# One of four weight sums moved from VectorE to GpSimd, and one product cut in two, in a decoder layer's MLP

## The reference

```python
u = rmsnorm(x, g_mlp[l]) @ w_up[l]
x = x + jnp.square(jax.nn.relu(u)) @ w_down[l]
return rmsnorm(x, g_final)
```

## Time and profile before

| | us |
|---|---|
| median of 3 runs | 415.57 (415.13 to 416.92) |
| the profiled execution, its own time | 416.76 |
| its span, first to last instruction | 415.0 |
| TensorE busy | 405.4 |
| VectorE busy | 333.9 |
| ScalarE busy | 250.4 |
| GpSimd busy | 27.0 |
| granted TensorE clock, mean share of full | 0.995 |

### The profile page before, as it was taken

How to read it: one execution, slowest core, us unless ns; L and a number is a source line. 1 busy time by engine, 2 the same in 40 slices (tenths; PEclk the granted TensorE clock), 3 DMA queues, 4 the chain that set the end, 5 groups by cost and what they waited for, 6 DMA issues and landing times.

```text
span 415.0 us, 7057 instructions
## 1 busy us (share of the span) xinstructions
PE 405.4 (98%) x2839; PEld 374.0 (90%) x2839; DVE 333.9 (80%) x441; ACT 250.4 (60%) x295; POOL 27.0 (6%) x40
## 2 busy tenths in 40 slices
PE   8999999999999999999999999999999999999993
PEld 7999988999999999889988899999999999999982
DVE  4788556977765737874858888999999999999976
ACT  5763337865665634551556648777777777777743
POOL 0079100000000000000200000000000000000003
PEclk9999999999999999999999999999999999999997
DMA  8999653534325255555453245555655555555002
GB/s 271 421 421 404 208 202 117 196 114 186 109 96 203 103 204 203 202 181 175 153 183 122 101 149 204 197 203 200 203 205 202 197 201 198 200 205 227 2 0 101
DMA packets 12107, 77.47 MB, mean 187 GB/s; under 512 B 1328, under 2 KB 1328, under 8 KB 3632
## 3 DMA queue, kind: packets, MB, share of 16 engines
q1 hardware_dynamic: 12080, 77.09, 51.7%
HBM read 76.04 MB, written 1.05 MB: 186 GB/s over the span
## 4 chain that ended last, share of the span: by engine, by line
PE 94%; DVE 2%; DMA 1%; ACT 1%; issue 0%; POOL 0%; SPq 0%; POOLq 0%; DVEq 0%; ACTq 0%
PE bank L1152 41%; PE bank L1447 16%; PE bank L1171 16%; PE bank L1288 11%; PE bank L1202 2%; PE bank L1300 1%; DVE res L1087 1%; DMA head_all<-in_pair_dram 1%; PE bank L1393 1%; PE bank L1413 1%; PE bank L1185 1%; PE bank L1341 1%; PE bank L1326 0%; PE bank L1406 0%; PE bank L1264 0%
## 5 line engine op out<-in xcount | busy, mean ns | idle before, releaser
L707 DVE TENSOR_TENSOR w_lo<-raw,w_hi 128x2048 fp32r<-128x2048 f32 (+2 forms) x83 | 145.0, 1753 | 26.5 <-ACT w_hi L455 25.2
L1152 PE MATMUL bank<-hT_hi,w_hi 128*128 128x256 f32 x384 | 108.2, 282 | 0.4 <-DVE hT_lo L719 0.4
L1152 PE MATMUL bank<-hT_hi,w_lo 128*128 128x256 f32 x384 | 107.8, 281 | 0.0
L1152 PE MATMUL bank<-hT_lo,w_hi 128*128 128x256 f32 x384 | 107.8, 281 | 0.0
L455 ACT ACTIVATE w_hi<-raw 128x2048 fp32r<-128x2048 f32 x33 | 62.8, 1915 | 29.9 <-PE bank L1152 15.2
L1152 PEld LDWEIGHTS bank<-hT_hi,w_hi 128*128 128x128 f32 x384 | 72.2, 188 | 1.2 <-issue 0.6
L1152 PEld LDWEIGHTS bank<-hT_hi,w_lo 128*128 128x128 f32 x384 | 73.2, 191 | 0.0
L1152 PEld LDWEIGHTS bank<-hT_lo,w_hi 128*128 128x128 f32 x384 | 72.4, 189 | 0.6
L707 DVE TENSOR_TENSOR t_lo<-t_sum,t_hi 128x1024 fp32r<-128x1024 f32 x30 | 36.2, 1208 | 0.0
L1288 PE MATMUL bank<-hT_hi,w_hi 128*128 128x256 f32 x128 | 35.8, 279 | 0.0
L1288 PE MATMUL bank<-hT_lo,w_hi 128*128 128x256 f32 x128 | 35.4, 277 | 0.0
(11 more groups left out here) (206 smaller groups left out, 848.9 us busy)
## 6 DMA issues: line engine op xcount, KB each, us to landing
raw<-in_weights_dram SPq DMA_DIRECT2D x65, 1024.0 KB, 4.8
head_all<-in_triples_dram SPq DMA_DIRECT2D x6, 384.0 KB, 6.7
raw<-in_chunk_dram SPq DMA_DIRECT2D x2, 512.0 KB, 8.3
res<-in_x_dram SPq DMA_DIRECT2D x2, 512.0 KB, 12.1
mem_tok<-in_mem_dram SPq DMA_DIRECT2D x1, 1024.0 KB, 11.9
memT_raw<-in_memT_dram SPq DMA_DIRECT2D x1, 1024.0 KB, 10.7
out_dram<-xs SPq DMA_DIRECT2D x2, 512.0 KB, 2.6
gfin<-in_g_final_dram SPq DMA_DIRECT2D x1, 512.0 KB, 5.8
```

Source lines behind the costliest of these rows:

```text
L707: return nc.vector.tensor_tensor(dst, whole, high.bitcast(fp32), sub)
L1152: last = mm(outs[m], w, v[:, k0 + k, :], start=first and n == 0, stop=k == nk - 1 and n == 2, skip_group_check=bool(kt_wait))
```

## The change

GpSimd gets the instruction `sum_t4` for every u = 0 to 14, with a semaphore of its own, `t4_made`; it waits until T2 is made. VectorE's `sum_t4` goes, and `t_made` counts two sums for a chunk instead of three. ScalarE's `high_t24`, and VectorE's `low_down` for B21 and `low_t24`, now wait for `t4_made`. In `down`, the last of the 21 matmuls (low part of S4 by high part of B22) is issued as two matmuls of 256 columns each, with the same stationary operand.

```diff
+            def sum_t4(u, i=0):
+
+                pool.wait_ge(t_made, 2 * PER * i + (2 * u + 2))
+                c = down_chunk(u)
+                nc.gpsimd.tensor_tensor(t_sum[:, u % 2, H * T4:H * T4 + H], raw[:, c % RAW, H * B21:H * B21 + H],
+                                        t_sum[:, u % 2, H * T2:H * T2 + H], ALU.add).then_inc(t4_made, 1)
+
+            sum_t4(0)
+            sum_t4(1)
+            with pool.Fori(0, ITERS) as i:
+                for u in range(2, 2 + PER):
+                    sum_t4(u, i)
+            sum_t4(PAIRS - 2)
...
             def high_t24(u, i=0):
 
-                act.wait_ge(t_made, 3 * PER * i + (3 * u + 3))
+                act.wait_ge(t4_made, PER * i + (u + 1))
...
-            def low_down(u, a, b, made, i=0):
+            def low_down(u, a, b, i=0, t4=False):
 
                 c = down_chunk(u)
                 dve.wait_ge(down_hi, PER * i + (u + 1))
-                dve.wait_ge(t_made, 3 * PER * i + made)
+                if t4:
+                    dve.wait_ge(t4_made, PER * i + (u + 1))
+                elif u < PAIRS - 1:
+                    dve.wait_ge(t_made, 2 * PER * i + (2 * u + 2))
...
             def mlp_rest(u, i=0):
                 low_up(u + 1, i)
-                sum_t4(u, i)
-                low_down(u, B11, B22 + 1, 3 * u + 2, i)
+                low_down(u, B11, B22 + 1, i)
                 low_t13(u, i)
                 form_s31(u, i)
-                low_down(u, B21, B21 + 1, 3 * u + 3, i)
+                low_down(u, B21, B21 + 1, i, t4=True)
...
                     for j, (s, w) in enumerate(((sh, wh), (sh, wl), (sl, wh))):
-                        last = mm(bank[p], s, w[:, n * H:n * H + H], start=start and j == 0,
-                                  stop=u == PAIRS - 2 and p in (P1, P6, P7) and j == 2, skip_group_check=True)
+                        for a, e in (((0, H),) if (p, j) != (P3, 2) else ((0, H // 2), (H // 2, H))):
+                            last = mm(bank[p][:, a:e], s, w[:, n * H + a:n * H + e], start=start and j == 0,
+                                      stop=u == PAIRS - 2 and p in (P1, P6, P7) and j == 2, skip_group_check=True)
```

More of the change, by code:

```diff
@@ L310, in hybrid_layer @@
         t_made, t13_hi, t24_hi, t_lo_done = sem("t_made"), sem("t13_hi"), sem("t24_hi"), sem("t_lo_done")
+        t4_made = sem("t4_made")
         u_relu, u_sq, s_made, f_hi_done, f_lo_done = (sem(n) for n in ("u_relu", "u_sq", "s_made", "f_hi_done",
@@ L617, in high_t13 @@
             def high_t13(u, i=0):
-                act.wait_ge(t_made, 3 * PER * i + (3 * u + 1))
+                act.wait_ge(t_made, 2 * PER * i + (2 * u + 1))
                 if u >= 2:
@@ L951, in sum_t13, with sum_t2 @@
                     .then_inc(t_made, 1)
-            def sum_t(u, t, b, t_in, made, i=0):
+            def sum_t2(u, i=0):
                 c = down_chunk(u)
-                dve.wait_ge(t_made, 3 * PER * i + made)
[L957 to L964, removed]
+                dve.wait_ge(t_made, 2 * PER * i + (2 * u + 1))
+                nc.vector.tensor_tensor(t_sum[:, u % 2, H * T2:H * T2 + H], raw[:, c % RAW, H * B22:H * B22 + H],
+                                        t_sum[:, u % 2, H * T1:H * T1 + H], ALU.add).then_inc(t_made, 1)
             sum_t13(0)
@@ L971, in _ @@
             for p in range(2):
-                if p == 1:
-                    sum_t4(0)
                 dve.wait_ge(xo_hi, p + 1)
@@ L996, in low_t13 @@
                 dve.wait_ge(t13_hi, PER * i + (u + 1))
-                dve.wait_ge(t_made, 3 * PER * i + (3 * u + 2))
+                dve.wait_ge(t_made, 2 * PER * i + (2 * u + 2))
                 low(t_lo[:, u % 2, 0:2 * H], t_sum[:, u % 2, 0:2 * H], t_hi[:, u % 2, 0:2 * H]).then_inc(t_lo_done, 1)
@@ L1002, in low_t24 @@
                 dve.wait_ge(t24_hi, PER * i + (u + 1))
-                dve.wait_ge(t_made, 3 * PER * i + (3 * u + 3))
+                dve.wait_ge(t4_made, PER * i + (u + 1))
                 low(t_lo[:, u % 2, 2 * H:4 * H], t_sum[:, u % 2, 2 * H:4 * H], t_hi[:, u % 2, 2 * H:4 * H])\
@@ L1053, in _ @@
                 low_T(X2, k, hT_hi, hT_lo, G_MLP)
-            low_down(0, B11, B22 + 1, 2)
+            low_down(0, B11, B22 + 1)
             low_t13(0)
-            low_down(0, B21, B21 + 1, 3)
+            low_down(0, B21, B21 + 1, t4=True)
             low_t24(0)
@@ L1069, in _ @@
             mlp_step(u)
-            low_down(u + 1, 0, 2, 3 * u + 3)
+            low_down(u + 1, 0, 2)
             low_forms(u)
             u = PAIRS - 1
-            low_down(u, 2, 4, 3 * u)
+            low_down(u, 2, 4)
             dve.wait_ge(x2_sumsq, TOK)
```

## The result

The changed kernel takes **424.61 us** (median of 5 runs, 424.51 to 426.20) against 415.57 us (five runs, 414.82 to 416.92), a ratio of 1.0225, 95% interval 1.0205 to 1.0244. It is slower, as forecast, but by 9.0 us where 3.8 us were forecast. The profiled execution took 425.84 us with a span of 424.1, 9.1 more than the 415.0 of before.

The account below looks back on a forecast made before the run. TensorE was taken to bound the kernel at 10.41 us a step, with VectorE at 10.29. 13 x 0.48 - 0.61 = 5.63 us, less the 1.80 lead, gave 415.57 + 3.8 = 419.4 us; range 416.8 to 430.5.

Parts of the forecast that it names:

- What bounds it: MLP steps: TensorE sets the pace at 10.41 us a step, VectorE follows at 10.29; the change passes the pace to VectorE.
- lead: Before down(14): low_forms(14) ends 1.83 us ahead, of which 1.80 us can be used up before TensorE starts later.
- The collision: Full MLP steps: GpSimd's sum holds VectorE's 1024-column low_down, lengthening it from 1.21 to some 2.3 us.
- The price: After low_up ends at E, GpSimd enters; VectorE loses 1.09 us and saves 0.61, net +0.48 us a step.
- rival 1: VectorE keeps the port until it waits for the sum before B21's low_down: +1.28 us a step, 429.8 us; chance 0.29.
- a mixture: The sum gets in at a later place of the step; time between the forecast and rival 1; chance 0.03.
- the forecast's case: GpSimd gets in when low_up ends in all 13 full steps: +0.48 us each, down(14) 3.8 us later; chance 0.49.
- u = 1: MLP's start: the sum uses VectorE's idle place, low_forms(0) reads 0.8 us later, counted as the saved 0.61 us.
- The halves: Last product of each down chunk as two 256-column matmuls: 0.009 us more each, +0.13 us on TensorE for 15 chunks.
- Rivals 2 and 3: GpSimd's hold is short and hidden, 415.7 to 416.5 us, chance 0.17; or VectorE's saving reaches the end, faster, chance 0.02.
- rival 2: MLP steps: VectorE loses less than 0.80 us a step and stays ahead of TensorE, 415.7 to 416.5 us; chance 0.17.

Follow-up runs that it names:

- experiment 3: Changed kernel with GpSimd's fourth sum replaced by a memset of the same 512 columns, which reads nothing, and GpSimd's loop written out: 413.7 us, 0.9935.
- experiment 5: Changed kernel with a two-column VectorE memset, without SBUF input, between low_up and the 1024-column low_down: 420.38 us, 1.0113.
- Experiments 1, 2 and 6: Changed kernel with GpSimd's sum in odd steps only, in even steps only, or also waiting for low_up's end: 420.59, 421.37 and 426.54 us.
- Experiment 9: Changed kernel with VectorE waiting for the end of low_forms(u-1) before the second sum: 423.42 us, 1.0184.
- odd_steps: Changed kernel with the fourth sum on GpSimd for odd u only, on VectorE for even u: 420.59 us, 1.0099.
- even_steps: Changed kernel with the fourth sum on GpSimd for even u only, on VectorE for odd u: 421.37 us, 1.0129.
- sum_only: Changed kernel with the last product of each down chunk whole again, the sum still on GpSimd: 424.3 us, 1.0219.
- experiment 7: Changed kernel without the halves, one matmul of 512 columns again, the sum still on GpSimd: 424.3 us, 1.0219.
- experiments 8 and 12: Kernel before with the last down product halved and two 256-column products of the first projection cut into 128 and 128; measured twice: 0.9980, 0.9968.

## Why the prediction was wrong, point by point

**What bounds it** was right: TensorE by 0.12 us a step, the pace passing to VectorE, a lead used up first. The lead was 1.68 us and not 1.80: the hand-over from f_lo to down(u), put at 0.03 us, is 0.15.

**The collision** was right: low_down takes 2.31 us instead of 1.21 beside the sum, and experiment 3, where GpSimd reads nothing, has no such instruction.

**The step that failed** is the one after it, in "The price": "it is held until E + 1.17 - 0.15", that GpSimd gets in when low_up ends, and with it "low_forms(14) moves by 13 x 0.48". It gets in there in 6 of the 13 full steps; in 7 VectorE's queue goes straight on, as rival 1 says. The chances treated the two as alternatives for all steps, 0.49 and 0.29, and gave 0.03 to a mixture, and that one was of another kind (a later place). What made the prediction choose it was a row taken for more than it shows. It took the price from the earlier trace rows, where GpSimd comes in at the end of a two-input subtraction. VectorE's timeline of the kernel before shows what stood behind that subtraction, with the same instruction once more at a time when GpSimd is idle:

```profile
33.42 0.68 DVE L782 SCALAR_TENSOR_TENSOR qkT<-bank,rstd_row 128x512 f32<-128x512 f32 x1
...
45.22 0.68 DVE L782 SCALAR_TENSOR_TENSOR qkT<-bank,rstd_row 128x512 f32<-128x512 f32 x1
```

It reads one input from PSUM (`bank`, the memory that TensorE writes its products to) and one from SBUF. It takes 0.68 us with GpSimd beside it (33.42) and without (45.22). Four subtractions there (from 28.32, 31.12, 34.03 and 37.08 us) hold up a GpSimd instruction, each has such an instruction behind it, and each time GpSimd comes in, done 0.26 to 0.28 us behind the subtraction's end. So the earlier trace rows are no contest between GpSimd and a waiting two-input instruction; they are nearer to experiment 5. Of the rows that the prediction used, only the earlier trace rows have an instruction with two SBUF inputs next in line, and there GpSimd stayed out, as rival 1 had said. That both outcomes occur in turn could not be read from the rows of before.

**The sizes of both cases were nearly right.** Let in: +0.48 forecast, +0.49 measured, 3.27 us against "about 3.3", low_down 2.31 against "some 2.3". Shut out: +1.28 forecast, +1.13 measured (+1.43 for the last), 5.88 us against "about 5.7". Experiment 5 makes the forecast's case in all steps, and gives down(14) + 3.82 us where 3.8 was forecast, with the luck said there. With the measured shares, the prediction's own two prices give 7 x 1.28 + 6 x 0.48 - 2.4 = 9.4 us, against 9.0; the price of the long case that is 0.15 too high and the lead that was 0.12 us shorter than the sum has it pull in opposite directions.

**Why they alternate.** A sum that is shut out makes VectorE wait, and the next sum is let in; one that is let in causes no wait, and the next is shut out. Experiments 1, 2 and 6 fit this: it doesn't go by buffer, by turn, by place or by the moment of asking. The step of a shut-out sum holds three waits: the 1.25 us for the sum, 0.13 us in front of low_t24 and 0.08 us in front of the next low_forms. They always come together, so the alternation alone can't say which of them counts. Experiment 9 says that a short one close by is enough: 0.12 to 0.15 us (0.04 in the last step) between low_forms and the second sum, and 13 of 13 are let in without any 1.25 us. The 0.08 us stands one instruction further back and is the nearest of the three, so it is the likelier cause; no run has it alone. Experiment 5 shows that an instruction without SBUF inputs in between is enough for 13 of 13, in an unbroken run. That VectorE hands the port from one queued instruction to the next when its queue has run ahead is the mechanism that I would argue; no run shows the queue. Three sums (u = 3 of odd_steps, u = 4 of even_steps, u = 10 of sum_only) were let in after a step without a wait, and why is open.

**u = 1** was right in its sum and wrong in one row: the saving is 0.61 us (261.80 to 261.19). low_forms(0) was expected to read 0.8 us later and is 1.91 us long instead of 1.09, the same hold in another form. VectorE's timeline:

```profile
250.09 1.91 DVE L722 TENSOR_TENSOR f_lo<-forms,f_hi 128x896 fp32r<-128x896 f32 x1 [0.42 <-ACT f_hi L657]
```

**The halves** were wrong in sign, without weight for this kernel: forecast +0.13 us in all, measured -0.19 us for each up section (5.46 against 5.65) and +0.02 for each down section, a TensorE step of 10.24 us instead of 10.41. The sum priced the two halves and took the spacing of the products behind them as given. In the changed kernel this saving disappears behind VectorE (experiment 7).

**Rivals 2 and 3** fell with the first VectorE instruction of 2.31 us: it is 1.10 us longer than usual, where rival 2 needed less than 0.80. There was no place in the step for GpSimd's reads beside VectorE's, as the prediction held.

## What to carry to other kernels

Work given to GpSimd is not free when VectorE runs two-input SBUF instructions without a break: a 512-column sum that saved 0.61 us of VectorE cost 1.10 us of it when it was let in, and more when it was shut out until VectorE needed its result. If it must be there, put a VectorE instruction that reads nothing from SBUF where GpSimd should enter (0.06 us here, 4.2 us better), or one that takes one of its two inputs from PSUM (let in at 4 of 4 places early in the kernel before), or give it a place where VectorE idles anyway (1.3 us, no loss). Before a row serves as the pattern for a collision, look at what stands next in the queue there. And where two outcomes are possible, price the mixture, and ask whether each outcome sets up the other.

## What the hardware did that was not expected

- A two-input VectorE queue of four instructions held a GpSimd instruction of 1.27 us for 4.6 us (5.88 less 1.27), past three places between two instructions, and an instruction of 0.06 us without SBUF inputs between two of them ended this in 13 of 13 steps.
- In the MLP's steps the 48 products of 256 columns have one of two spacings throughout: 0.1177 us (5.65/48) after a full 512-column product, 0.1137 us (5.46/48) after two halves of it. A cut at the other end of the down section changes nothing (5.65/48).
- This is no rule for other places. In the kernel before itself, 48 such products right behind full 512-column ones take 5.47 us; the first six come 0.12 us apart, the rest at the narrower spacing. TensorE's chain there:

```profile
65.13 10.99 PE bank L1171 x48
76.13 5.47 PE bank L1288 x48
```

- The stream at the kernel's head, from 26 to 51 us, of which there is one profiled execution for each experiment, ran at the narrower spacing in both with the cut of experiments 8 and 12 (24.64 and 24.62 us for 217), but also in two of the twelve without it (24.50 and 24.51 us for 216; the others 25.44 or 25.45). What sets the spacing is open.
